# Layer tail: the first norm, its transposes and the first feed-forward blocks, one token half after the other

## What is computed

```python
x = layer_norm(DEEPNORM_ALPHA * x + (1 + gate[0][:, None]) * y.astype(x.dtype), ln_g[i, 0], ln_b[i, 0])   # y: the mixer's output projection
h = x * (1 + scale[1][:, None]) + shift[1][:, None]
y = swiglu(h, ffn_w_in[i], ffn_w_out[i])        # 2816 hidden features
x = layer_norm(DEEPNORM_ALPHA * x + (1 + gate[1][:, None]) * y.astype(x.dtype), ln_g[i, 1], ln_b[i, 1])
```

## Time and profile before

| | |
|---|---|
| median of 3 runs | 2398.78 us (2398.62 to 2403.65) |
| the profiled execution | 2401.94 us, its span 2400.2 us |
| PE busy | 2269.9 us, 95% of the span, 12021 matmuls |
| DVE busy | 1813.9 us, 76% |
| ACT busy | 1151.0 us, 48% |
| POOL busy | 131.4 us, 5% |
| DMA | 572.53 MB, mean 239 GB/s |

### The profile page before, as it was taken

The page is one execution under the profiler, slowest core; times in us unless marked ns, Lnnn a source line. Parts: engine busy times, 40 slices in busy tenths (PEclk is TensorE's granted clock), DMA queues, the critical chain, the costliest instruction groups (busy, mean ns, idle before and its releaser), DMA issues. The chain is left out here.

```text
span 2400.2 us, 30431 instructions
## 1 busy us (share of the span) xinstructions
PE 2269.9 (95%) x12021; PEld 1919.0 (80%) x12021; DVE 1813.9 (76%) x2133; ACT 1151.0 (48%) x1197; POOL 131.4 (5%) x229
## 2 busy tenths in 40 slices
PE   7999888899999999989999999999999999898997
PEld 7889667788888888877788787887887788797886
DVE  6887676588888889856788767887676888777545
ACT  4443234466767677734444363442642443364342
POOL 2000100000000000000011001110001111000000
PEclk9999988999999999999999999999999999999999
DMA  8843552499999999954699436994624898344552
GB/s 303 274 134 119 180 169 86 123 361 367 367 361 369 356 371 355 361 168 156 195 384 353 157 124 195 384 360 148 202 93 136 266 371 310 125 142 158 193 193 71
DMA packets 347058, 572.53 MB, mean 239 GB/s; under 512 B 68128, under 2 KB 181280, under 8 KB 346912
## 3 DMA queue, kind: packets, MB, share of 16 engines
q1 hardware_dynamic: 326176, 495.02, 61.0%
q0 software_dynamic: 20736, 75.51, 8.4%
HBM read 569.39 MB, written 1.05 MB: 238 GB/s over the span
## 5 line engine op out<-in xcount | busy, mean ns | idle before, releaser
L286 DVE TENSOR_TENSOR st_lo<-st_raw,st_hi 128x2048 fp32r<-128x2048 f32 (+1 forms) x195 | 441.0, 2267 | 139.1 <-ACT st_hi L276 138.9
L286 DVE TENSOR_TENSOR es_lo<-es_raw,es_hi 128x2048 fp32r<-128x2048 f32 x192 | 429.2, 2285 | 76.6 <-ACT es_hi L276 75.3
L276 ACT CAST st_hi<-st_raw 128x2048 fp32r<-128x2048 f32 (+1 forms) x195 | 368.2, 1892 | 244.1 <-PE ps L316 177.3
L314 PE MATMUL ps<-st_hi,sb_h_hi 128*128 128x512 f32 (+1 forms) x1232 | 464.7, 377 | 15.3 <-DVE sb_h_lo L1115 7.9
L316 PE MATMUL ps<-st_hi,sb_h_lo 128*128 128x512 f32 (+1 forms) x1232 | 454.5, 369 | 0.0
L315 PE MATMUL ps<-st_lo,sb_h_hi 128*128 128x512 f32 (+1 forms) x1232 | 454.2, 369 | 0.0
L276 ACT CAST es_hi<-es_raw 128x2048 fp32r<-128x2048 f32 x192 | 357.5, 1910 | 51.1 <-DMA es_raw<-in_w_expert_up_dram 25.8
L314 PEld LDWEIGHTS ps<-st_hi,sb_h_hi 128*128 128x128 f32 x1232 | 235.4, 191 | 57.8 <-issue 14.0
L316 PEld LDWEIGHTS ps<-st_hi,sb_h_lo 128*128 128x128 f32 x1232 | 234.7, 190 | 39.2
L315 PEld LDWEIGHTS ps<-st_lo,sb_h_hi 128*128 128x128 f32 x1232 | 235.5, 191 | 35.8
L314 PE MATMUL ps<-es_hi,moe_hg_hi 128*128 128x512 f32 x512 | 205.9, 402 | 5.3 <-PEq L61 5.3
(11 more groups left out here) (690 smaller groups left out, 3768.1 us busy)
## 6 DMA issues: line engine op xcount, KB each, us to landing
st_raw<-in_ffn_w_in_dram SPq DMA_DIRECT2D x176, 512.0 KB, 6.3
t_aw<-in_ada_w_dram POOLq DMA_DIRECT2D x144, 512.0 KB, 7.0
es_raw<-in_w_expert_gate_dram SPq DMA_DIRECT2D x64, 1024.0 KB, 8.2
es_raw<-in_w_expert_up_dram SPq DMA_DIRECT2D x64, 1024.0 KB, 7.4
es_raw<-in_w_expert_down_dram SPq DMA_DIRECT2D x64, 1024.0 KB, 7.3
st_raw<-in_ffn_w_out_dram SPq DMA_DIRECT2D x44, 1024.0 KB, 8.2
fb_aw<-in_ada_w_dram SPq DMA_DIRECT2D x39, 512.0 KB, 5.9
hs_raw<-in_w_in_dram SPq DMA_DIRECT2D x36, 512.0 KB, 6.9
```

The source lines that it names most:

```text
L276: act.copy(p.at(self.hi[:, m % self.held, :]), p.at(self.raw[:, n % self.slots, :])).then_inc(self.high, 1)
L286: dve.tensor_tensor(p.at(self.lo[:, m % self.held, :]), p.at(self.raw[:, n % self.slots, :]), p.at(self.hi[:, m % self.held, :]).bitcast(F ...
L314: pe.matmul(out, a_hi, b_hi, start=start, stop=False, skip_group_check=True)
```

## The change

At site 0 the norm, transposes, scaling and splitting go half by half. PE finishes both column parts of half 0 first, transposes half 0 (turn_half, into banks 4 and 5; half 1 into 6 and 7) around the last product group of half 1, and runs half 0 through f0, f1 and the start of f2 (opened) before half 1's transposes; then half 1 through the same three pieces. DVE's order becomes: both adds of half 0, its moments, add(0,1,0), normalise 0, f0's low part, the split of half 0 (divide_half), f1's low part, add(0,1,1), moments, f2's low part, normalise 1, the split of half 1. ACT makes sixteen 128x128 tiles in place of eight 128x256. There is no stir at site 0. SP's column loads wait for the eighth split in place of the fifth. turn_norm keeps only site 1, with stir under `if t and i == 0`.

```diff
             if not final:
-                sp.wait_ge(hs, len(SPLITS))
+                sp.wait_ge(hs, 8)
...
-            def turn_norm(site, t):
+            def turn_half(t):
+                pe.wait_ge(gated, 2 + 2 * t)
                 for i in range(8):
-                    if i == 0 and t == (not site and not early):
+                    if i % 4 == 0:
+                        pe.wait_ge(normed, 2 * t + i // 4 + 1)
+                    last = pe.transpose(ps[:, 4 + 2 * t + i // 4, i % 4 * P:(i % 4 + 1) * P], y[:, t, i * P:(i + 1) * P],
+                                        k.ident[:])
+                    if i % 4 == 3:
+                        last.then_inc(turned2, 1)
+            def turn_norm(t):
+                for i in range(8):
+                    if t and i == 0:
                         stir(k, pe, 0, 9)
                     if i % 4 == 0:
-                        pe.wait_ge(normed, 4 * site + 2 * t + i // 4 + 1)
+                        pe.wait_ge(normed, 4 + 2 * t + i // 4 + 1)
                     at = i % 2 * T + t * P
-                    last = pe.transpose(ps[:, turn_bank(i), at:at + P], (y, X)[site][:, t, i * P:(i + 1) * P], k.ident[:])
+                    last = pe.transpose(ps[:, turn_bank(i), at:at + P], X[:, t, i * P:(i + 1) * P], k.ident[:])
...
             if early:
                 out_part(1, 1, k.early, 0).then_inc(S.used, 1)
-                for c in range(2):
-                    w = S.take(pe)
-                    pe.wait_ge(xs, 2)
-                    out_part(0, c, w, 4).then_inc(part, 1)
-                    out_part(1, c, w, 4).then_inc(S.used, 1)
+                w = S.take(pe)
+                pe.wait_ge(xs, 2)
+                out_part(0, 0, w, 4).then_inc(part, 1)
+                v = S.take(pe)
+                out_part(0, 1, v, 4).then_inc(part, 1)
+                out_part(1, 0, w, 4).then_inc(S.used, 1)
+                out_part(1, 1, v, 4).then_inc(S.used, 1)
+                turn_half(0)
             else:
                 w = S.take(pe)
                 pe.wait_ge(xs, 2)
@@ -929,15 +943,14 @@
                 w = S.take(pe)
                 pe.wait_ge(xs, 4)
                 out_part(0, 0, w, 4).then_inc(part, 1)
+                u = S.take(pe)
+                out_part(0, 1, u, 0)
+                v = S.take(pe)
+                out_part(0, 1, v, 4).then_inc(part, 1)
                 out_part(1, 0, w, 4).then_inc(S.used, 1)
-                w, v = S.take(pe), S.take(pe)
-                out_part(0, 1, w, 0)
-                out_part(0, 1, v, 4).then_inc(part, 1)
-                out_part(1, 1, w, 0).then_inc(S.used, 1)
+                out_part(1, 1, u, 0).then_inc(S.used, 1)
+                turn_half(0)
                 out_part(1, 1, v, 4).then_inc(S.used, 1)
-            pe.wait_ge(gated, 3)
-            turn_norm(0, 0)
-            turn_norm(0, 1)
...
+            def opened(b, w, t, kts):
+                at = slice(t * P, (t + 1) * P)
+                for kt in kts:
+                    pe.wait_ge(hs, 4 * t + kt // 2 + 1)
+                    last = product(pe, ps[:, b * 2 + t, :], h_hi[:, kt, at], h_lo[:, kt, at], w[0][:, kt % 4, :],
+                                   w[1][:, kt % 4, :], kt == 0, kt == 7)
+                return last
+            w = S.take(pe)
+            opened(0, w, 0, range(0, 4))
+            u = S.take(pe)
+            opened(0, u, 0, range(4, 8))
+            v = S.take(pe)
+            opened(1, v, 0, range(0, 2))
+            turn_half(1)
+            opened(1, v, 0, range(2, 4))
+            opened(0, w, 1, range(0, 4)).then_inc(S.used, 1)
+            opened(0, u, 1, range(4, 8)).then_inc(S.used, 1)
+            opened(1, v, 1, range(0, 4)).then_inc(S.used, 1)
+            turn_hidden(0)
+            for kind, b, a in order[3:-2]:
...
-            S.lift(act, o + 5)
-            def modulated(site):
+            S.lift(act, o + (6 if early else 5))
+            def modulated_half(t):
+                at = slice(t * P, (t + 1) * P)
                 for i in range(8):
-                    act.wait_ge(turned2, 4 * site + i // 2 + 1)
+                    act.wait_ge(turned2, 2 * t + i // 4 + 1)
                     if i >= 4:
-                        act.wait_ge(hs, len(SPLITS) * site + splits_for(i - 4))
+                        act.wait_ge(hs, 4 * t + (i - 4) // 2 + 1)
+                    act.activation(full[:, i % 4, at], ps[:, 4 + 2 * t + i // 4, i % 4 * P:(i % 4 + 1) * P], ACT.Identity,
+                                   scale=k.cols[:, 1, 2, i:i + 1], bias=k.cols[:, 1, 3, i:i + 1]).then_inc(scaled, 1)
+            def modulated():
+                for i in range(8):
+                    act.wait_ge(turned2, 4 + i // 2 + 1)
+                    if i >= 4:
+                        act.wait_ge(hs, 8 + splits_for(i - 4))
                     act.activation(full[:, i % 4, :], ps[:, turn_bank(i), i % 2 * T:(i % 2 + 1) * T], ACT.Identity,
-                                   scale=k.cols[:, 1 - site, 2, i:i + 1], bias=k.cols[:, 1 - site, 3, i:i + 1]
-                                   ).then_inc(scaled, 1)
-            modulated(0)
+                                   scale=k.cols[:, 0, 2, i:i + 1], bias=k.cols[:, 0, 3, i:i + 1]).then_inc(scaled, 1)
+            modulated_half(0)
+            S.lift(act, f0 + 3)
+            modulated_half(1)
...
+            def divide_half(t):
+                cols = slice(t * P, (t + 1) * P)
+                for q in range(4):
+                    at, buf = slice(2 * q, 2 * q + 2), full[:, 2 * q % 4:2 * q % 4 + 2, cols]
+                    dve.wait_ge(scaled, 8 * t + 2 * q + 2)
+                    dve.tensor_copy(h_hi[:, at, cols], buf).then_inc(hh, 1)
+                    dve.wait_ge(hh, 4 * t + q + 1)
+                    dve.tensor_tensor(h_lo[:, at, cols], buf, h_hi[:, at, cols].bitcast(F32), ALU.subtract
+                                      ).then_inc(hs, 1)
+            def divide():
                 for q, (a, z) in enumerate(SPLITS):
                     at, buf = slice(a, z), full[:, a % 4:a % 4 + z - a, :]
-                    dve.wait_ge(scaled, 8 * site + z)
+                    dve.wait_ge(scaled, 16 + z)
                     dve.tensor_copy(h_hi[:, at, :], buf).then_inc(hh, 1)
-                    dve.wait_ge(hh, len(SPLITS) * site + q + 1)
+                    dve.wait_ge(hh, 8 + q + 1)
                     dve.tensor_tensor(h_lo[:, at, :], buf, h_hi[:, at, :].bitcast(F32), ALU.subtract
                                       ).then_inc(hs, 1)
             dve.wait_ge(part, 1)
             add(0, 0, 0)
-            dve.wait_ge(S.used, o + (3 if early else 2))
-            add(0, 1, 0)
-            S.lower(dve, f0 + 1)
             dve.wait_ge(part, 2)
             add(0, 0, 1)
             moments(0, 0)
-            if not early:
-                normalise(0, 0)
+            dve.wait_ge(S.used, o + (3 if early else 2))
+            add(0, 1, 0)
+            normalise(0, 0)
+            S.lower(dve, f0 + 1)
+            divide_half(0)
+            S.lower(dve, f0 + 2)
             dve.wait_ge(S.used, o + 4)
             add(0, 1, 1)
             moments(0, 1)
-            if early:
-                normalise(0, 0)
+            S.lower(dve, f0 + 3)
             normalise(0, 1)
-            divide(0)
+            divide_half(1)
```

More of the change, by code:

```diff
@@ L947, in gate_up @@
                 for kt in range(a, a + 4):
-                    if b == 0:
-                        pe.wait_ge(hs, splits_for(max(kt, 1)))
                     for t in range(NT):
@@ L989, in ada_gate @@
                           start=True, stop=True).then_inc(ada_rows, 1)
-            for kind, b, a in order[:-2]:
+            def opened(b, w, t, kts):
[18 more added lines that the diff above has]
+            for kind, b, a in order[3:-2]:
                 if kind != "D":
@@ L1028, in _ @@
                 pe.wait_ge(merged, 1)
-                turn_norm(1, 0)
-                turn_norm(1, 1)
-                ready = lambda kt: (hs, len(SPLITS) + splits_for(kt))
+                turn_norm(0)
+                turn_norm(1)
+                ready = lambda kt: (hs, 8 + splits_for(kt))
                 (open_features if layer == 1 else open_tokens)(k, pe, ready)
@@ L1068, in _ @@
                 act.wait_ge(merged, 1)
-                modulated(1)
+                modulated()
         @block.vector
@@ L1107, in scale_row @@
                 after(dve.tensor_tensor(X[:, t, :], X[:, t, :], lnr[:, 1, :], ALU.add))
-            def divide(site):
+            def divide_half(t):
[8 more added lines that the diff above has]
+            def divide():
                 for q, (a, z) in enumerate(SPLITS):
                     at, buf = slice(a, z), full[:, a % 4:a % 4 + z - a, :]
-                    dve.wait_ge(scaled, 8 * site + z)
+                    dve.wait_ge(scaled, 16 + z)
                     dve.tensor_copy(h_hi[:, at, :], buf).then_inc(hh, 1)
-                    dve.wait_ge(hh, len(SPLITS) * site + q + 1)
```

(3 more changed lines are left out.)

## The result

| | before | after |
|---|---|---|
| median of 12 runs each | 2400.12 us (2397.46 to 2409.72) | 2410.1 us (2402.13 to 2421.31) |
| the profiled execution | 2401.94 us, span 2400.2 | 2412.59 us, span 2410.8 |

The account below looks back on a forecast made before the run. PE, busy 95% of the span, bounds the kernel; only its idle or low-clock places give time. Site 0 +1.1, stir +5.9 and clock +3.9 sum to +10.9 us on the 2398.78 median: 2409.7 us, range 2402 to 2416.

Parts of the forecast that it names:

- The signs named in advance: Site 1: ACT's first tile 3.2 to 3.6 us later, clock 0.5; site 0: waits 2 to 3 us, loads 3.5 later.
- the three signs of being wrong: Layers 0, 2: way to hidden transposes shrinks over 3 us; site 1 stir free; PE waits over 3 us for f6-f8.
- Stir on the path: Site 1, layers 0 to 2: stir's 18 matmuls between the halves cost 1.96 us each, +5.9 us.
- The clock at site 1: Site 1: after 3.36 us idle PE's clock falls, costing 1.3 us (0 to 1.7) at each of three sites, +3.9 us.
- Site 0's order, as written out by hand: Site 0 at full clock: layers 0 and 2 -1.1 us each, layers 1 and 3 +0.1 each; PE idles 2.8, 2.1.
- The clock at site 0: Site 0, layers 0 and 2: falls mostly hit products ending in a wait; 0 taken, at most 1.6 us each.
- The small ACT tile: Site 0: ACT's 128x128 tile takes 0.37 us, between 0.36 and the wide tile's 0.47.
- The term for late DMA: Site 0: column loads start later, so f6 leaves 2.6 to 3.7 us later; brings site 0 to +1.1 us.
- My upper end: Site 0 with f6 3.7 us late: layers 0 and 1 each 2.5 us later than in the new order.
- DMA late at its price: Rival: PE waits for f6 and f8 at site 0, plus one clock fall; +16.9, 2415.7 us, chance 0.12.
- Faster: Rival: PE meets no hole at f1 and f2 at site 0; -10.4, 2388 us, chance 0.06.
- No fall: Rival: the clock holds at site 1 and only stir costs there; +5.9 + 1.1, 2405.8 us, chance 0.20.

Follow-up runs that it names:

- the kernel before moved: Kernel before the change, only site 1's stir moved between the two halves: 2417.79 us, ratio 1.0049; run again 2414.56 us, ratio 1.0042.
- the early cast: Changed kernel with ACT casting f1 ahead of half 0's eight tiles in layers 0 and 2 too: 2410.85 us, ratio 1.0039.
- the doubled loads: Changed kernel with the eight column loads issued twice in layers 0 to 2: 2464.98 us, ratio 1.0248.
- both repairs: Changed kernel with site 1's stir back ahead of half 0's transposes and f1 cast before the eight tiles: 2396.7 us, 0.9971; again 2398.49 us, 0.9979.

## Why the prediction was right, step by step

- **Size and sign: right.** Predicted +10.9 us, span +10.6; 2409.7 us, median 2410.1. By the ratio of all runs the change costs 8.4 us. Several terms were off and made up for each other, below.
- **The signs named in advance.** ACT's first tile at site 1 came 3.28 us later (3.2 to 3.6 forecast), with stir between the transposes and a clock of 0.50. PE's waits at site 0 were to be 2 to 3 us each and were 2.41 and 1.67 in layer 0; the column loads began 2.5 us later, not 3.5. None of the three signs of being wrong appeared.
- **Stir on the path: right in place and mechanism, a little too dear.** 1.96 predicted, 1.77 to 1.79 measured, three times: +5.3 for +5.9. The runs don't say which 0.2 us of it lies beside other work. The kernel before with this one condition moved is 0.42% slower, the change itself 0.35% and 0.41%; undoing it leaves no loss.
- **The clock at site 1: right as a mean, wrong as a constant, and the upper bound too low.** Predicted 1.3 at each of three sites, 3.9. Over five executions (the first profile after, its repetition, the kernel before moved, the early cast, the doubled loads with ways of 6.51 / 6.95 / 6.38) it was 5.9, 0, 3.3, 6.2 and 4.5 us, mean 4.0. Single falls cost 1.40 to 1.65 us, except in layer 2, 2.73 and 2.93 in two of them, where I had put "at most 1.7": this row of the windows after, at layer 2's site 1, shows the clock low through nearly all of stir, not only its first part.

```profile
2075.00:2077.00 2.00, 2.00 (x12) 2.00 (x12) 0.00 (x0) 0.00 (x0) 0.00 (x0) 0.56 0.00 0
```

- **Site 0's order, as written out by hand: right in shape.** PE waits for the low parts of f1 and f2, 2.41 and 1.67 us in layer 0 (2.8 and 2.1 predicted). The way from the first product on (1141.8) to the hidden transposes shrank from 47.38 to 45.22 us; 0.9 of that is a fall of the clock at the layer's entry in the profile before that the one after didn't have, the rest, -1.3, stands for the predicted -1.1. Layer 2 gained 0.61; there the fall at the entry covers eleven matmuls after and seven before, 0.8 us more, so its order gave about 1.4. Layers 1 and 3 were to lose 0.1 each and lost 0.15 and 0.12. (Layer 1 before had two more idles than the one of 1.53 that I named: 1.29 ahead of its transposes and 0.62 ahead of f1.) Layer 1 has the stops that I gave it as 1.4, 1.9 and 2.1:

```profile
1468.25 0.47 PE L314 MATMUL ps<-st_hi,sb_h_hi 128*128 128x512 f32 x1 [1.34 <-DVE sb_h_lo L1157]
...
1472.75 0.50 PE L314 MATMUL ps<-st_hi,sb_h_hi 128*128 128x512 f32 x1 [1.52 <-DVE st_lo L286]
...
1477.43 0.50 PE L314 MATMUL ps<-st_hi,sb_h_hi 128*128 128x512 f32 x1 [1.67 <-DVE st_lo L286]
```

- **The clock at site 0: right, and seen.** I took 0 because most of a fall would lie on products that end in a wait. After f1's hole the clock did fall in layer 2, and in the second profile of the changed kernel in layers 0 and 2. Two rows of that profile, layer 0: f1's products are slow (0.63 us for 0.39), and the wait for f2 is 0.19 in place of 1.67.

```profile
1175.71 0.63 PE L316 MATMUL ps<-st_hi,sb_h_lo 128*128 128x512 f32 x1
1176.53 0.50 PE L314 MATMUL ps<-st_hi,sb_h_hi 128*128 128x512 f32 x1 [0.19 <-DVE st_lo L286]
```

  Layer 0's way is 47.93 us with this fall and 47.94 without.
- **The small ACT tile: right.** 0.37 us each taken; four took 1.50, and this row of the tile t_full (least, middle and most ns of one) makes that 0.35 from one to the next, (1.50 - 0.46) / 3:

```profile
L1079 ACT ACTIVATE t_full<-ps,cols x64: 447/457/465, 1162.0 to 2221.8; 128x128 f32<-128x128 f32 x64
```

  Half the columns cost three quarters of the time (0.47 for the wide tile), so sixteen take 5.6 us for 3.8 before, and f1's cast stands behind eight of them.
- **The term for late DMA: the one that failed, by its size.** "f6 goes out 2.6 to 3.7 us later" turned a site 0 of -2.0 us (twice -1.1, twice +0.1) into +1.1; measured, site 0 is -2.5. SP's queue after, then before:

```profile
1170.21 0.92 SPq L254 DMA_DIRECT2D st_raw<-in_ffn_w_in_dram  x2
1181.06 0.37 SPq L858 DMA_DIRECT2D cols<-in_ada_b_dram  x1
1181.47 1.04 SPq L858 DMA_DIRECT2D cols<-in_ln_g_dram  x1
...
1188.73 0.98 SPq L254 DMA_DIRECT2D st_raw<-in_ffn_w_in_dram  x2
```

```profile
1177.60 0.92 SPq L254 DMA_DIRECT2D st_raw<-in_ffn_w_in_dram  x2
...
1179.11 3.73 SPq L858 DMA_DIRECT2D cols<-in_ln_g_dram  x1
```

The loads did begin 2.5 us later (1181.06 for 1178.57), but they held the queue for 7.7 us instead of 10.1 (8.7 for 11.3 in layer 1, 9.0 for 9.9 in layer 2), and in layer 0 f6 left within 0.1 us of its old time. I had taken their duration as fixed. Most of the difference is the first load of ln_g: 3.6 to 3.8 us at all six places in the profiles of the old order, where a weight piece is sent just ahead of the loads, and 1.0 to 1.5 at all 27 places in the new order, where the piece is sent 11 us ahead. That the piece is the cause is not tested by itself.

PE is ahead as well, though. Counted from PE's first hidden transposes f6 left 2.4, 1.7 and 4.0 us later than before in layers 0, 1 and 2, as I had feared. What absorbed it is slack. The low part of f6 was ready 3.6 / 0.9 / 3.6 us before PE took it in the profile before and 1.3 / 1.3 / 0.06 after; in layer 1 its transfer took 8.4 us instead of 11.0 up to ACT's cast, which made up for the later start. Layer 2, to which I had given the larger slack of layer 0, is the tight one. The row of f6's low part there, then PE's first product with it:

```profile
1902.42 2.29 DVE L286 TENSOR_TENSOR st_lo<-st_raw,st_hi 128x2048 fp32r<-128x2048 f32 x1 [1.34 <-ACT st_hi L276]
```

```profile
1904.77 0.50 PE L314 MATMUL ps<-st_hi,sb_h_hi 128*128 128x512 f32 x1
```

In the second profile with stir alone put back, the wait that I had priced did happen, in layer 2: ACT, then PE.

```profile
1886.17 1.91 ACT L276 CAST st_hi<-st_raw 128x2048 fp32r<-128x2048 f32 x1 [8.02 <-DMA st_raw<-in_ffn_w_in_dram]
```

```profile
1890.46 0.50 PE L314 MATMUL ps<-st_hi,sb_h_hi 128*128 128x512 f32 x1 [1.60 <-DVE st_lo L286]
```

That is one wait of 1.60 us at 24 places (eight profiles with the new order and single loads), where the sum had 3.1 us in every execution. My upper end wasn't even consistent: 3.7 us late less slacks of 1.3 and 0.8 is 2.4 and 2.9, not 2.5 twice. In the profile after, this is all that PE waited for from 1180 to 1365 us, for a hidden tile and no weight piece, and the same single 0.5 stands in layers 1 and 2:

```profile
PE ps L999 <- DVE t_hid_lo L1189: 0.5, 1, 0.5
```

- **The rivals.** DMA late at its price, +16.9, is refuted; its mechanism is real, at the edge in layer 2. "Faster" failed at the point the prediction named, f1's low part. "No fall" is what one of the two executions of the changed kernel did, and its span still was 8.9 us above the one before: stir 5.3, site 0 -2.6, and 6.2 in stretches where the change edits nothing, 4.0 of it in the mixer after layer 1. Totals of single executions can't decide this rival; the ways at site 1 do.

That the total came so close is partly luck. Predicted: site 0 +1.1, site 1 +9.8, the rest 0. Measured: -2.5, +11.2 and +1.9. The DMA term and stir's price were too dear, the falls of this one execution and the mixers filled the gap. The 1.14 us in the mixer after layer 1 are small beside what this stretch does anyway: it took 151.5 to 160.3 us over the eleven profiles, whichever the kernel, and the part of the program ahead of layer 0's tail took 1133 to 1143.

## What to carry to other kernels

A filler on the tensor engine is worth what its place makes of it: ahead of a wait it is free, behind one it is on the path at full price, and dearer where the clock is low. The same holds for a fall of the clock: on products that end in a wait it cost nothing here, on the path 0.9 to 2.9 us. When a loop's condition is rewritten for a special case, compare in the trace where every instruction under it lands in the other cases too. Splitting a norm by halves doesn't remove a hole if the engine that feeds both halves also lowers the weights between them: write out that engine's queue first, and put the cast it waits for ahead of the small tiles. Before calling a later transfer harmless, look at the slack in every layer, and not only in the first.

## What the hardware showed beside that

- The clock fell or held at the same place, after the same 3.28 to 3.29 us of idle, in one execution or another of one program: 3 of 3 sites in the profile after, 0 of 3 when it ran again. The Trainium skill (TensorE: Matmul & The Clock Gate, Part 1) says that the activity monitor runs free of the kernel's start; these rows agree. With stir back ahead of the transposes it fell at none of twelve sites (four profiles), although has a fall behind idles of only 1.00 and 1.52.
- The eight small column loads held the queue for 7.2 to 15.1 us over the profiles, and the same load of ln_g's column took 1.04 us in one order and 3.73 in the other, so small loads can't be priced from one profile.
- Stretches that no edit touched differ between profiles by as much as the change costs: the mixer after layer 1 by 8.8 us (151.54 with both repairs, 160.31 without any stir at site 1).
